# Sampled attention of a decoder step: selected-block values moved behind the token scores, packing of the next tokens moved behind the dilated maximum

## The reference

```python
kg, vg = kb[bi, hi, idx], vb[bi, hi, idx]            # selected blocks of 64 rows, an own set for each query token
p = softmax(mask(q @ kg * SCALE)); o_slc = p @ vg
o_win = window_attend(q, k_win, v_win)               # the last 512 rows
for g, (w, d) in enumerate(((128, 1), (512, 4), (2048, 16))):
    o, lse = dilated_group(q_b[g], k_dil[g], v_dil[g], w, d)   # mixed by softmax over the three lse
```

## Time and profile before

| | us |
|---|---|
| median of 3 runs | 1597.9 (1595.86 to 1598.83) |
| profiled execution, its own time | 1598.45 |
| its span in the trace | 1596.6 |
| TensorE busy in the span | 1486.3 (93%) |
| VectorE busy | 728.4 (46%) |
| ScalarE busy | 553.3 (35%) |
| GpSimd busy | 173.8 (11%) |

### The profile page before, as it was taken

The page is one execution under the profiler, slowest core; times in us unless marked ns, Lnnn a source line. Parts: engine busy times, 40 slices in busy tenths (PEclk is TensorE's granted clock), DMA queues, the critical chain, the costliest instruction groups (busy, mean ns, idle before and its releaser), DMA issues.

```text
span 1596.6 us, 29276 instructions
## 1 busy us (share of the span) xinstructions
PE 1486.3 (93%) x12329; PEld 1373.7 (86%) x12331; DVE 728.4 (46%) x1197; ACT 553.3 (35%) x906; POOL 173.8 (11%) x194
## 2 busy tenths in 40 slices
PE   2999999999999999999988978887889999999998
PEld 2788879999999999999875656776879999999998
DVE  4789975334323346345445553332663333233331
ACT  2443443223133422333424555555234432122211
POOL 4334200000000000000051005440000000000000
PEclk9999999999999999999968997888889999999999
DMA  8654413435344454242313008883213333133331
GB/s 244 232 191 165 153 52 119 145 131 162 128 154 158 122 175 138 77 165 82 110 45 92 3 27 237 242 240 116 58 49 94 91 89 109 54 96 88 89 109 56
DMA packets 192413, 195.00 MB, mean 122 GB/s; under 512 B 10902, under 2 KB 172509, under 8 KB 191773
## 3 DMA queue, kind: packets, MB, share of 16 engines
q1 hardware_dynamic: 171045, 111.64, 23.4%
q0 software_dynamic: 16928, 81.76, 15.5%
q10 hardware_dynamic: 4352, 0.34, 0.2%
HBM read 188.49 MB, written 31.40 MB: 138 GB/s over the span
## 4 chain that ended last, share of the span: by engine, by line
PE 86%; DVE 5%; ACT 3%; issue 2%; DMA 2%; POOL 2%; SPq 0%; ACTq 0%; DVEq 0%; POOLq 0%
PE PS L857 20%; PE PS L859 20%; PE PS L858 20%; PE PS L805 3%; PE PS L806 3%; PE PS L807 3%; PE PS L1188 3%; PE PS L1152 1%; PE PS L1263 1%; PE PS L1134 1%; PE PS L1208 1%; PE PS L837 1%; PE PS L1113 1%; DVE QTR L1834 1%; DMA BIG<-in_cache_cmp_kv,IXC 1%
## 5 line engine op out<-in xcount | busy, mean ns | idle before, releaser
L857 PE MATMUL PS<-HNH,WHI 128*128 128x272 f32 x1408 | 408.2, 290 | 7.8 <-DVE HNL L1838 6.6
L858 PE MATMUL PS<-HNL,WHI 128*128 128x272 f32 x1408 | 406.3, 289 | 0.0
L859 PE MATMUL PS<-HNH,WLO 128*128 128x272 f32 x1408 | 405.8, 288 | 0.0
L857 PEld LDWEIGHTS PS<-HNH,WHI 128*128 128x128 f32 x1408 | 266.5, 189 | 11.6 <-issue 8.1
L859 PEld LDWEIGHTS PS<-HNH,WLO 128*128 128x128 f32 x1408 | 267.2, 190 | 0.0
L858 PEld LDWEIGHTS PS<-HNL,WHI 128*128 128x128 f32 x1408 | 267.1, 190 | 0.0
L1743 DVE TENSOR_TENSOR WLO<-WR,WHI 128x1024 fp32r<-128x1024 f32 (+3 forms) x144 | 192.4, 1343 | 156.9 <-ACT WHI L1367 156.1
L1367 ACT ACTIVATE WHI<-WR 128x1024 fp32r<-128x1024 f32 (+3 forms) x144 | 164.6, 1151 | 278.7 <-DMA WR<-in_ffn_in 129.9
L857 PE MATMUL PS<-HIDH,WHI 128*128 128x272 f32 x704 | 202.4, 287 | 0.0
L859 PE MATMUL PS<-HIDH,WLO 128*128 128x272 f32 x704 | 202.4, 287 | 0.0
L858 PE MATMUL PS<-HIDL,WHI 128*128 128x272 f32 x704 | 201.9, 287 | 0.0
(11 more groups left out here) (381 smaller groups left out, 2341.8 us busy)
## 6 DMA issues: line engine op xcount, KB each, us to landing
WR<-in_ffn_in SPq DMA_DIRECT2D x88, 512.0 KB, 3.7
WR<-in_ffn_out SPq DMA_DIRECT2D x32, 704.0 KB, 4.3
out_dil_s<-in_cache_dil_kv POOLq DMA_DIRECT2D x8, 2044.0 KB, 9.1
WR<-in_w_in SPq DMA_DIRECT2D x14, 648.0 KB, 4.4
BIG<-in_cache_dil_kv SPq DMA_DIRECT2D x8, 512.0 KB
WR<-in_w_out SPq DMA_DIRECT2D x8, 512.0 KB, 3.8
out_dil_s<-in_cache_dil_kv POOLq DMA_DIRECT2D x8, 508.0 KB, 5.2
out_win_s<-in_cache_win_kv POOLq DMA_DIRECT2D x8, 508.0 KB, 5.2
```

The lines of the kernel that those rows point to most:

```text
L857: pe.matmul(out, a[0], b[0], start=first, stop=False)
L858: pe.matmul(out, a[0], b[1], start=False, stop=False)
L859: return pe.matmul(out, a[1], b[0], start=False, stop=last)
```

## The change

No instruction is added or taken away; the order of four engines' work in a sequence changes, and OEA gets a second buffer.

- TensorE: ED(b - 1) is turned right behind EW(b - 1), ahead of the token scores. EA, ES, key 4 and the selected values of b stand right behind the window and dilated values of b - 1. Key 0 of b + 1 comes last.
- ScalarE: copies of EA and ES come behind OEB(b - 1), ahead of the copies of keys 4 and 5; OEA follows, ahead of the copies of keys 6 and 7.
- VectorE: packs 0 and 1 of b + 1 come behind shift_b and pads; the sum and reciprocal of branch B (`sums_b`) move between packs 2 and 3 of the next sequence.
- The table TURN has EA and ES behind ED, and OEA alternates between two places in DEC.

```diff
@@ TURN
             names += [("EW", b - 1), ("ED", b - 1)] if b else []
+            names += [("EA", b), ("ES", b)] if b < NB else []
             names += [("T", b, x) for x in range(4, 8)] if b < NB else []
             names += [("F", b - 1)] if b else []
-            names += [("EA", b), ("ES", b)] if b < NB else []
             names += [("T", b + 1, 0)] if b + 1 < NB else []
@@ TensorE, back(b)
-                turns(("F", b), [OEA] + [OEB[:, g * P:(g + 1) * P] for g in range(3)], P)
+                turns(("F", b), [OEA[b % 2]] + [OEB[:, g * P:(g + 1) * P] for g in range(3)], P)
@@ TensorE, the loop over b
                 if b:
                     exps_w(b - 1)
+                    exps_d(b - 1)
                 if b < NB:
                     token_scores(b)
-                if b:
-                    exps_d(b - 1)
-                if b < NB:
-                    keys(b, 4)
                 if b:
                     wd_values(b - 1)
...
                 if b < NB:
+                    pe.wait_ge(sa["expa"], b + 1)
+                    turns(("EA", b), [EA[:, SEL7 * j:SEL7 * j + SEL7 + TS] for j in range(4)], P)
+                    turns(("ES", b), [EA[:, SC1:SC1 + P]], P)
+                    keys(b, 4)
+                    slc_values(b)
                     keys(b, 5)
                     scores(b, 4)
                     keys(b, 6)
...
                     scores(b, 7)
-                    pe.wait_ge(sa["expa"], b + 1)
-                    turns(("EA", b), [EA[:, SEL7 * j:SEL7 * j + SEL7 + TS] for j in range(4)], P)
-                    turns(("ES", b), [EA[:, SC1:SC1 + P]], P)
                     if b + 1 < NB:
                         keys(b + 1, 0)
-                    slc_values(b)
@@ ScalarE, the loop over b
                 if b < NB:
                     exps_a(b)
-                    keys_copied(b, 4)
-                    keys_copied(b, 5)
                 if b:
                     act.wait_ge(sa["pvb"], b)
                     act.wait_ge(sa["rib"], b)
...
                 if b < NB:
+                    name = ("EA", b)
+                    R = SEL7 + TS
+                    copied(name, ETA[0:R, :, :].rearrange("p j c -> p (j c)"), turn_bank(name)[0:R, :])\
+                        .then_inc(sa["copied"], 1)
+                    name = ("ES", b)
+                    copied(name, ETS, turn_bank(name)[:, 0:P]).then_inc(sa["copied"], 1)
+                    keys_copied(b, 4)
+                    keys_copied(b, 5)
+                    act.wait_ge(sa["pva"], b + 1)
+                    act.wait_ge(sa["ria"], b + 1)
+                    for t in range(TS):
+                        r = slice(32 * t, 32 * t + 6)
+                        last = act.activation(OEA[b % 2][r, :], PS[r, 6, t * P:(t + 1) * P], ACT.Copy,
+                                              scale=RIA[r, :])
+                    last.then_inc(sa["oea"], 1)
                     keys_copied(b, 6)
                     keys_copied(b, 7)
...
                     if b + 1 < NB:
                         keys_copied(b + 1, 0)
                     exps_b(b)
-                    act.wait_ge(sa["pva"], b + 1)
-                    act.wait_ge(sa["ria"], b + 1)
...
-                    last.then_inc(sa["oea"], 1)
@@ VectorE
+            def sums_b(b):
+                dve.wait_ge(sa["expb"], b + 1)
+                link(V.tensor_reduce(SUB[:, 2:3], SUB[:, 0:2], AX.X, ALU.add))
+                V.reciprocal(RIB[0:40, :], SUB[:, 2:3]).then_inc(sa["rib"], 1)
...
             for b in range(NB):
                 pack(b, 2)
+                if b:
+                    sums_b(b - 1)
                 pack(b, 3)
                 shift_a(b)
                 dve.wait_ge(sa["expa"], b + 1)
                 V.reciprocal(RIA, SUA).then_inc(sa["ria"], 1)
-                if b + 1 < NB:
-                    pack(b + 1, 0)
-                    pack(b + 1, 1)
                 shift_b(b)
                 if b + 1 < NB:
                     pads(b + 1)
-                dve.wait_ge(sa["expb"], b + 1)
-                link(V.tensor_reduce(SUB[:, 2:3], SUB[:, 0:2], AX.X, ALU.add))
-                V.reciprocal(RIB[0:40, :], SUB[:, 2:3]).then_inc(sa["rib"], 1)
+                    pack(b + 1, 0)
+                    pack(b + 1, 1)
+            sums_b(NB - 1)
```

More of the change, by code:

```diff
@@ L424, in build @@
         ETS = DEC[:, 6720:6848]
-        OEA, OEB, VN, ETD = DEC[:, 6592:6720], DEC[:, 7104:7488], DEC[:, 7616:8128], DEC[:, 8128:9280]
+        OEA, OEB, VN, ETD = [DEC[:, 6592:6720], DEC[:, 6848:6976]], DEC[:, 7104:7488], DEC[:, 7616:8128], DEC[:, 8128:9280]
         ZEROS = DEC[:, 5600:9280]
@@ L1657, in _ @@
                 if b < NB:
[L1658 to L1663, removed]
                     if b + 1 < NB:
@@ L1666, in _ @@
                     exps_b(b)
-                    act.wait_ge(sa["pva"], b + 1)
-                    act.wait_ge(sa["ria"], b + 1)
-                    for t in range(TS):
-                        r = slice(32 * t, 32 * t + 6)
-                        last = act.activation(OEA[r, :], PS[r, 6, t * P:(t + 1) * P], ACT.Copy, scale=RIA[r, :])
-                    last.then_inc(sa["oea"], 1)
             act.wait_ge(sa["pva"], NB)
```

## The result

The changed kernel took 1637.84 us (median of four runs, 1635.73 to 1640.98); the kernel before, beside it on the same chip, 1596.88 (four runs, 1595.38 to 1598.83). The ratio is 1.0257, with a 95% interval of 1.0235 to 1.0279: 41 us slower. The profiled execution took 1640.98 us around a span of 1639.2. In the kernel after, the lines behind the edits have other numbers: VectorE's packs are L2159, shift_b L2200 to L2206, pads L2177 to L2183, sums_b L2210 and L2211; ScalarE's copies are L1591, exps_a L1604, exps_b L1609 and L1611, OEB L1639 and L1640, OEA L1655. The kernels of the experiments differ from these by a few lines more.

The account below looks back on a forecast made before the run. The prediction took the VectorE to ScalarE to VectorE chain to set each sequence's end. Six times (2.5 + 2.9), plus 4.4 plus 2.2, made 39.0 us on 1598.45: 1637.5 us, range 1617 to 1658.

Parts of the forecast that it names:

- What bounds it: In the attention stage, the VectorE to ScalarE to VectorE chain sets each sequence's end; TensorE then waits 1.77 us for pack 2.
- S: The end of L1215, the last dilated score of a sequence, from which the prediction times the sequence's end.
- S to the next token scores, 7.1 to 9.6: End of a sequence: late packs and key 0's copy delay exps_b, thirteen transposes follow; cost 2.5 us per sequence.
- Token scores to S, 11.6 to 14.5: First part of a sequence: slower window values and new waits for ScalarE's copies; cost 2.9 us per sequence.
- The clock in the middle, counted at nothing: TensorE's new wait of about 0.8 us ahead of the selected values was given no clock cost in the sum.
- rival B: The clock falls again in mid-sequence, 1666 us, or stays low through the window values, 1648; chance 0.18.
- Transfers, counted at nothing: Loads of selected blocks gain lead and the longer pace lowers DMA need, so no cost was counted.
- First transition, +4.4: From sequence 0 to 1, without window values: 21.7 us where it took 17.3, cost 4.4 us.
- Last sequence, +2.2: Sequence 7: first part costs 2.9 us, 0.7 comes back behind it, cost 2.2 us.
- A: Rival: the clock stays as high as before or higher, about 19 us more, about 1617 us; chance 0.10.
- C: Rival: TensorE's own work is the bound and the change wins, pace 17.0, kernel 1586 us; chance 0.04.
- D: Rival: the reorder moves nothing that ends last, new waits hide in each other, 1598 us; chance 0.02.

Follow-up runs that it names:

- experiment 1: The changed kernel with VectorE's packs 0 and 1 of the next sequence put back ahead of shift_b: 1619.54 us, ratio 1.0133.
- experiment 2: The changed kernel with ScalarE's exps_b ahead of the copy of the next sequence's key 0: 1622.2 us, ratio 1.0159.
- experiment 8: The kernel before, with VectorE's sums_b behind packs 2 and 3 and OEA moved ahead of the next sequence's exps_a: 1597.03 us, ratio 0.9988.
- experiment 12: The kernel of experiment 9 with nine unused 512-column matmuls ahead of key 2: 1591.63 us, ratio 0.9963 to the kernel before.
- experiment 10: The changed kernel with unused 512-column matmuls on TensorE, 13 behind the dilated scores and 5 ahead of key 3: 1618.03 us, ratio 1.012.
- experiment 9: The kernel of experiment 7 with packs 2 and 3 directly behind shift_b, pads and sums behind them: 1600.81 us, ratio 1.0008 to the kernel before.
- experiment 6: The changed kernel with ScalarE's OEA copies behind the copies of keys 6 and 7: 1630.14 us, ratio 1.0207.
- experiment 7: The changed kernel with packs 0 and 1 early, EA and ES copied ahead of OEB, OEA behind keys 6 and 7: 1615.07 us, ratio 1.0095.
- experiment 4: The kernel before, with VectorE's sums_b behind packs 2 and 3 of the next sequence: 1595.41 us, ratio 0.9984.

## Why the prediction was right, and where it was not

The forecast was 1637.5 us and the measurement 1637.84. The steps, in the prediction's order:

- **What bounds it.** Right. The chain from S through VectorE and ScalarE sets the end of a sequence, and edits to it alone (experiments 1 and 2) give back 18 and 16 us, in part by the clock.
- **S to the next token scores, 7.1 to 9.6.** Measured 9.70. The wait for pack 0 is 3.42 us for about 3.5; exps_b starts at 4.77 for 4.4, because TensorE turned key 0 at the low clock already; L2210 starts at 6.25 (1055.33 less 1049.08) for 5.9. The last link, thirteen transposes at 1.2 GHz, was then 2.7 us.
- **Token scores to S, 11.6 to 14.5.** Measured 14.24. The window values took 3.3 us for 3.8; the wait ahead of L1242 is 0.70 for about 0.8; that behind OEA is 0.57 for 0.3. Small errors against each other.
- **The clock in the middle, counted at nothing.** Right: the windows show 1.00 past the waits of 0.70 and 0.57 us, so rival B's second fall did not come. The Trainium skill, page "TensorE: Matmul & The Clock Gate", section "A second HAM failure mode: psum-queue depth-cycling", tells of a kernel of bf16 matmuls with 512 columns that idled briefly between groups, often enough for the clock to swing between its levels; it gives no rule for how often that is, and here two such idles in 14 us did not do it.
- **Transfers, counted at nothing.** Right for this kernel: the table of waits from sequence 1 to 7 lists none on a landing, and the share of the DMA engines over 990 to 1090 us fell from 0.84 to 0.72. It is no general truth: at 17 us per sequence they bind (experiments 8 and 12).
- **First transition, +4.4.** Wrong in size: +6.7. The working took EA, ES and the selected values at the full clock, but TensorE waits 2.11 us for the exponentials in the sequence without window values, and what follows ran at the low clock up to the window scores: the selected values took 1.94 us where 1.08 is usual, as the timeline of the kernel after shows.

```profile
966.41 1.27 PE L1188 MATMUL PS<-CO,DEC 128*84 128x128 f32 x5 [2.11 <-ACT DEC L1604]
...
968.46 1.94 PE L1242 MATMUL PS<-WR,DEC 80*32 80x128 f32 x32
```

- **Last sequence, +2.2.** The first part gave +2.2 instead of the 2.9; behind it I had promised 0.7 back, and 0.2 more was paid. The wait ahead of the first window value did fall by 0.7 (0.66 for 1.35), but the eight transposes of EW and ED ahead of it ran at the low clock, 1.97 us for 1.09 before, so that the value followed 6.62 us behind S for 6.44. The sum is 2.4.

```profile
1148.72 1.97 PE L1188 MATMUL PS<-CO,DEC 128*128 128x128 f32 x8 [4.00 <-ACT DEC L1611]
...
1151.35 0.85 PE L1258 MATMUL PS<-DEC 96*32 96x384 f32 x1 [0.66 <-ACT DEC L1591]
```

- **The sum.** 31.6 for 32.4, 6.7 for 4.4, 2.4 for 2.2: 40.7 for 39.0. The 1.9 us by which the stage began later were in nobody's working, and the median lies 3 us below the profiled execution. That the total came within 0.4 us of the median is luck on top of right terms.
- **The rivals.** A, the clock stays up, would have been 1617: when it was made to (experiment 10), the kernel took 1618. The price was right; what failed to come was the condition. C, TensorE's own work as the bound, would need the packs ready when TensorE comes to them; its waits of 3.42 us for pack 0 and 1.40 for pack 3 rule it out for this kernel, and even with the ends shortened (experiment 9) the changed order only equals the old one. D fell with the 4.77 us at L1609.

What stays open: what made the low clock shorter in experiment 6 and longer in experiment 7, and whether either order could run below 17 us with fewer bytes to gather, which was not tried.

## What to carry to other kernels

In an in-order queue the costly move is the one that puts an independent operation ahead of a critical one: VectorE's late packs cost little by TensorE's wait for them and much by the exponentials that stood behind the copy of their result, so for each step that is moved later, read who is queued behind its consumers on their engines. Price a wait of TensorE with the clock that follows it: here the low clock was worth 12 us before the change and 20 to 22 after it, and a few matmuls without a use in the longest wait, sized to end just before the awaited operand is there, gained more (12 us) than any reordering of the kernel before that was tried (2.5 us at best, experiment 4). Before shortening a chain further, look at the share of the DMA engines over the stage: at 0.84 there was one more step to be had, at 0.93 none was found.

## What was not expected of the hardware

A gather issued by GpSimd took longer in one place. Its usual row is 0.89 us; the one that ran from 1051.59 to 1052.96, beside VectorE's copies of pads (L2177 to L2183) and of the packs (L2159, 1051.96 to 1052.84), took 1.37, as the timeline of the kernel after has it:

```profile
1050.40 0.89 POOL L740 DMA_INDIRECT BIG<-in_cache_slc_kv,IXS  x1 [0.31 <-issue]
...
1051.59 1.37 POOL L740 DMA_INDIRECT BIG<-in_cache_slc_kv,IXS  x1 [0.30 <-issue]
```

It was so at the end of each of the first six sequences (1.35 to 1.37 us, the first 1.19). The packs alone do not do it: in the kernel before, a gather that began 0.15 us ahead of the same four copies (L2160, 1069.01 to 1070.05 in the earlier trace rows) and ran beside them took the usual time.

```profile
1068.86 0.89 POOL L740 DMA_INDIRECT BIG<-in_cache_slc_kv,IXS  x1 [0.30 <-issue]
```

It cost nothing here: from sequence 1 to 7 nothing waited for a landing. The Trainium skill, page "SBUF — State Buffer", section "SBUF: two separate sides", says that GpSimd can't write the descriptors of its DMAs while VectorE copies fp32 within SBUF in its fast mode. The row of the kernel after agrees in direction, with half a microsecond for one gather; the row of the kernel before shows no delay. Whether it is the copies of pads or which of the two engines began first that makes the difference, no run here shows.
